# Layer 0 of a two-layer trunk, from mixer to experts: C by SyncE, gate row a tile earlier, table turns behind the router, B tables behind the overflow row

## The reference, cut to what matters

```python
def reference(x, c, positions, ada_w, ada_b, ...):
    cond = jax.nn.silu(c)
    for layer in range(DEPTH):
        mod = cond @ ada_w[layer] + ada_b[layer]
        sh_m, sc_m, g_m, sh_f, sc_f, g_f = jnp.split(mod, 6, axis=-1)
        h = _modulate(_rmsnorm(x, norm_mix_g[layer]), sh_m, sc_m)
        if layer % 2 == 0:
            m = _attn_lru_mixer(h, positions, ...)
        else:
            m = _s5_mixer(h, ...)
        x = x + g_m[:, None, :] * m
        h = _modulate(_rmsnorm(x, norm_ffn_g[layer]), sh_f, sc_f)
        x = x + g_f[:, None, :] * _hier_moe(h, ...)
    return _rmsnorm(x, final_g)
...
    # in _s5_mixer: B is scaled by coefficients of the poles, C is used as it is
    bb_re = coef_re[..., None] * br - coef_im[..., None] * bi
    bu_re = jnp.einsum('bsgc,gpc->bsgp', u, bb_re)
    y = (jnp.einsum('bsgp,gcp->bsgc', h_re, c_re) - jnp.einsum('bsgp,gcp->bsgc', h_im, c_im) + d * u)
```

## Time and profile before

| | |
|---|---|
| median of 3 runs | 955.0 us (953.03 to 955.36) |
| the profiled execution's own time | 954.5 us |
| its span | 952.7 us, 12757 instructions |
| mean granted TensorE clock | 0.956 of full |
| TensorE matmul busy | 848.1 us (89%) |
| VectorE, ScalarE, GpSimd busy | 303.4, 191.3, 150.9 us |
| chain that ended last | TensorE 75%, VectorE 10%, DMA 7% |
| of it the load of C's imaginary part | 3% |
| HBM read | 279.50 MB, 299 GB/s over the span |

### The profile page before, as it was taken

The page is one execution under the profiler, slowest core; times in us unless marked ns, Lnnn a source line. Parts: engine busy times, 40 slices in busy tenths (PEclk is TensorE's granted clock), DMA queues, the critical chain, the costliest instruction groups (busy, mean ns, idle before and its releaser), DMA issues.

```text
span 952.7 us, 12757 instructions
## 1 busy us (share of the span) xinstructions
PE 848.1 (89%) x5229; PEld 463.9 (49%) x5230; DVE 303.4 (32%) x708; ACT 191.3 (20%) x310; POOL 150.9 (16%) x244
## 2 busy tenths in 40 slices
PE   3799998799999998999687999699999899999993
PEld 0367644565465553554544543434444554654641
DVE  1337432541130410311799610620000311301314
ACT  1403330421221311312400100310101212213111
POOL 3201019185443445300000000000000000000000
PEclk9799999789999999999799999789999899999997
DMA  9999999439999999996997682207775299999961
GB/s 306 346 382 276 343 384 360 164 130 400 392 399 402 393 398 400 392 392 245 395 337 263 214 310 87 98 2 259 275 261 186 106 398 392 396 397 391 393 248 68
DMA packets 126288, 285.32 MB, mean 299 GB/s; under 512 B 7092, under 2 KB 8388, under 8 KB 125992
## 3 DMA queue, kind: packets, MB, share of 16 engines
q1 hardware_dynamic: 119392, 276.83, 78.9%
q0 software_dynamic: 1984, 5.21, 1.9%
q10 hardware_dynamic: 4872, 2.72, 1.0%
HBM read 279.50 MB, written 5.24 MB: 299 GB/s over the span
## 4 chain that ended last, share of the span: by engine, by line
PE 75%; DVE 10%; DMA 7%; ACT 2%; issue 2%; SPq 2%; ACTq 1%; DVEq 0%
PE PS L1578 19%; PE PS L1597 13%; PE PS L1605 8%; PE PS L1621 7%; PE PS L1581 6%; PE PS L1866 5%; PE PS L1324 4%; PE PS L1418 3%; DMA yg<-in_s_c_im 3%; DMA ring<-in_moe_w 2%; DMA work<-in_ada_w 2%; PE PS L1349 2%; DVE work L1289 2%; PE PS L1401 2%; SPq L339 1%
## 5 line engine op out<-in xcount | busy, mean ns | idle before, releaser
L1597 PE MATMUL PS<-ring,work 128*64 128x512 f32 (+1 forms) x512 | 130.5, 597 | 6.2 <-ACT work L772 6.2
L1578 PE MATMUL PS<-ring,hT 128*64 128x256 f32 x896 | 108.4, 383 | 2.5 <-DMA ring<-in_moe_w 2.5
L1578 PE MATMUL PS<-ring,yg 128*64 128x256 f32 x896 | 107.4, 381 | 0.0
L1578 PEld LDWEIGHTS PS<-ring,hT 128*64 128x64 f32 x896 | 66.5, 137 | 40.0 <-issue 8.5
L1597 PEld LDWEIGHTS PS<-ring,work 128*64 128x64 f32 (+1 forms) x512 | 43.1, 143 | 85.4 <-issue 85.4
L1211 DVE TENSOR_TENSOR work<-work,PS 128x512 f32<-128x512 f32 x32 | 22.0, 687 | 194.9 <-PE PS L1578 146.9
L1605 PE MATMUL PS<-work,xhat 128*128 128x256 f32 (+1 forms) x256 | 76.9, 453 | 7.0 <-issue 6.9
L1578 PEld LDWEIGHTS PS<-ring,yg 128*64 128x64 f32 x896 | 68.1, 138 | 29.7 <-issue 0.9
L1215 DVE COPY yg<-PS 128x512 f32<-128x512 f32 x32 | 22.1, 692 | 180.5 <-PE PS L1597 180.5
L1621 PE MATMUL PS<-yg,grow 64*128 64x512 f32 (+1 forms) x256 | 70.1, 612 | 7.1 <-DVE yg L1215 7.1
L1605 PEld LDWEIGHTS PS<-work,xhat 128*128 128x128 f32 x256 | 49.2, 207 | 38.8 <-issue 22.1
(11 more groups left out here) (345 smaller groups left out, 978.3 us busy)
## 6 DMA issues: line engine op xcount, KB each, us to landing
ring<-in_moe_w SPq DMA_DIRECT2D x96, 2048.0 KB, 16.7
ring<-in_ada_w SPq DMA_DIRECT2D x20, 2048.0 KB, 15.0
work<-in_ada_w SPq DMA_DIRECT2D x4, 2048.0 KB, 13.8
ring<-in_s_glu_w SPq DMA_DIRECT2D x4, 2048.0 KB, 16.6
ring<-in_ab_w_in SPq DMA_DIRECT2D x3, 2048.0 KB, 21.9
ring<-in_ab_w_out SPq DMA_DIRECT2D x2, 2048.0 KB, 13.6
rot_tables<-work POOLq DMA_DIRECT2D x16, 256.0 KB, 5.7
ring<-rot_tables SPq DMA_DIRECT2D x2, 2048.0 KB, 11.1
```

The costliest lines, as they stand in the source:

```text
L1578: last = mm(dst[64 * u:64 * u + 64, 0:256], hg[k][:, e * P:e * P + 64], w[:, k, 256 * u:256 * u + 256], start=k == 0, stop=k == KD - 1)
L1597: last = mm(dst, heT[:, at:at + (64 if narrow else P)], w[:, c4, h * HALF:(h + 1) * HALF], start=c4 == 0, stop=c4 == KF - 1)
```

## The change

It moves work in layer 0 between the last closing tiles and the first gather, and nothing is added or left out but waits.

- SyncE issues the four loads of C, behind the last adaLN weights of the early part (and behind `pv_done` 6, when the memory is free), ahead of the first expert weights. ScalarE no longer does.
- `ada_cols(1)` and `gate_row(0)` stand one closing tile earlier, behind tile (0, 0) and (0, 1).
- `turn_tables(0, 4)` stands behind the router's columns and the first opening, into banks 0, 5, 2 and 3. Tables 2 and 3 wait for the copy of the second gate row (`grow_ready` 2). Bank 5 is that of accumulator 1, which is opened last, behind the copy of the tables (`tab_evac` 4); the router no longer waits for it.
- On ScalarE the second gate row is copied ahead of both exponentials, and the table copies behind them, in place of ahead of the norm.
- GpSimd makes the B tables behind `over_row(0)`.
- In layer 1 three banks instead of two are opened ahead of the rank matmuls, and the gate row is copied ahead of the exponentials.

```diff
-        TABLES = ((2, 0, 0, 6), (2, 0, 1, 7), (2, 1, 0, 4), (2, 1, 1, 5),
+        TABLES = ((2, 0, 0, 0), (2, 0, 1, 5), (2, 1, 0, 2), (2, 1, 1, 3),
...
@@ SyncE
                 send_ada(u)
+            sp_.wait_ge(S("pv_done"), 6)
+            for v, name in enumerate(("s5_c_re", "s5_c_im")):
+                for u in range(2):
+                    sp_.dma_start(Cn[:, v, :, u * 64:(u + 1) * 64],
+                                  a[name][0].rearrange("(k g) c p -> (g c) k p", k=KD)).then_inc(S("cn_in"), 16)
             for L in range(2):
                 n0 = MOE_BASE[L]
...
@@ GpSimd
+            over_row(0)
             for tab, c0 in ((G1, 3), (G0, 5)):
...
             pool.sem_inc(S("b_tables"), 1)
 
-
-            over_row(0)
             w32 = lambda m: Ew[:, m, :]
...
@@ ScalarE
             s.activation(lr_t[:, :, :], lr_t[:, :, :], ACT.Sqrt).then_inc(S("lru_a"), 1)
-            for v, name in enumerate(("s5_c_re", "s5_c_im")):
-                for u in range(2):
-                    s.dma_start(Cn[:, v, :, u * 64:(u + 1) * 64],
-                                a[name][0].rearrange("(k g) c p -> (g c) k p", k=KD)).then_inc(S("cn_in"), 16)
             rows_out(1)
             gate_row(0)
...
             def ffn(L):
                 n = 2 * L + 1
-                if L == 0:
-                    table_evac(0, 4)
-                else:
+                if L == 1:
                     s.activation(warm, ones[:, 0:1], ACT.Sqrt)
                 norm(n)
                 modulate(n)
+                gate_row(n)
                 act.wait_ge(S("lg_ready"), L + 1)
                 s.activation(exp_g.rearrange("p (b e) -> p b e", b=NB), sets_b(less)[:, :, 0, :], ACT.Exp).then_inc(
                     S("exp_ready"), 1)
-                gate_row(n)
                 act.wait_ge(S("l2_ready"), L + 1)
                 s.activation(exp_2, mx2, ACT.Exp).then_inc(S("exp_ready"), 1)
+                if L == 0:
+                    table_evac(0, 4)
...
@@ TensorE
             for b, h in tiles:
                 mix_out(b, h, LT, KD)
+                if (b, h) == (0, 0):
+                    ada_cols(1)
                 if (b, h) == (0, 1):
-                    ada_cols(1)
-                if (b, h) == (1, 0):
                     gate_row(0)
...
                     if n_ == 2:
-                        pe.wait_ge(S("grow_ready"), 1)
+                        pe.wait_ge(S("grow_ready"), 2)
...
-            turn_tables(0, 4)
             pe.wait_ge(S("x_new"), 1)
...
                 if L == 0:
                     pe.wait_ge(S("small_in"), 16 * 9)
-                    pe.wait_ge(S("tab_evac"), 4)
...
-                open_acc(0)
-                open_acc(1)
+                for m in (0,) if L == 0 else (0, 1, 2):
+                    open_acc(m)
+                if L == 0:
+                    turn_tables(0, 4)
                 pe.wait_ge(S("member_ready"), L + 1)
...
                 last.then_inc(S("rank_ps"), 1)
-                open_acc(2)
-                open_acc(3)
+                for m in (2, 3) if L == 0 else (3,):
+                    open_acc(m)
+                if L == 0:
+                    pe.wait_ge(S("tab_evac"), 4)
+                    open_acc(1)
                 pe.wait_ge(S("narrow_known"), L + 1)
```

## The result

The change takes **949.93 us** (median of 6 runs, 945.86 to 950.24) against 953.83 (6 runs, 952.47 to 955.36) for the kernel before: ratio **0.995**, 95% interval [0.993, 0.997]. A second series on another chip gave 947.89 (6 runs, 947.31 to 951.04), ratio 0.9947 [0.9929, 0.9966]. The profiled execution took 948.89 us with a span of 947.1 (before: 954.5 and 952.7). The forecast was 949.0 in a range of 945.5 to 952.5. The total was right, in part by luck. The kernel before measured 953.83 and not the 955.0 that the forecast set out from, so the gain is 3.9 us by the medians (5.4 in the second series), where 6.0 was forecast. In the profiles two errors work against each other: the first gather began 6.8 us earlier and not 5.2, and 3.2 us of that went again in the experts' stage, where nothing was to be lost.

A forecast was written before the change was run, and what follows sets the result against it. The bound was the chain of waits in layer 0 up to the first gather, including C's load (23.91 us). Gather 5.2 earlier plus 0.6 shorter: 954.5 - 5.8 = 948.7, with 0.5 to the median, rounded 949.0; range 945.5 to 952.5.

The forecast's parts named there:

- Residual, x, norm: Layer 0 behind the closing tiles: residual starts 3.6 us earlier, x ready 3.1 earlier, norm 5.8 earlier.
- C: C's loads on SyncE: landing between 149.8 and 172.5, wanted by TensorE at 176.7, so cost nothing.
- Router to gather: Layer 0, turned x to first gather: rank matmuls at 179.3, gather 5.2 us earlier and 0.6 shorter.
- From there to the end of the router's matmuls 8.2 us stay: From x's turns at 167.55, the router's matmuls take an unchanged 8.2 us, ending at 175.7.
- I expect the fall near 181.5: TensorE's clock falls to 0.50 near 181.5, after dense work ends at 178.7, during the openings.
- I take 185.0 for the gather's start: First gather of layer 0 starts at 185.0, 5.2 us earlier, between picks at 184.2 and openings at about 185.5.
- rival 1: The clock holds through openings and gather: gather at 184.2 in 8.11 us, gain 8.7, time 946.3 or 945.9; chance 0.08.
- Tables beside the first group: GpSimd's B tables beside VectorE's first-group work: cost nothing, at worst 1 us, from 0.36 an operation for three operations.
- GpSimd's end: GpSimd's last work of layer 0 moves to about 403, needed some 459: cover of 56 us, cost nothing.
- The experts' stage: Weights' stream starts when the first slot is freed, so equally earlier: no loss, bounds plus and minus 0.5 us.
- Layer 1: One more opening ahead of rank matmuls, gate row ahead of the exponential: taken 0, bounds 1.9 gained, 0.3 lost.
- The sum: Whole kernel: 954.5 less 5.8 makes 948.7, with 0.5 to the median and rounded 949.0.

The follow-up runs named there:

- experiment 8: Kernel before, with only the four table turns, their copies and the openings moved behind the router (layer 1 as in the change): 949.82 us, ratio 0.9962.
- experiment 7: The change with B tables held until the first group's weights are turned, gate row and its columns back in their old place: 948.87 us, ratio 0.9948.
- Experiment 6: The change, with C's loads issued by ScalarE as before instead of SyncE: 949.91 us, ratio 0.9967.
- Experiment 9: Openings' zero products over 128 rows instead of one: 942.55 us on the change with B tables held (945.90 without), 950.23 on the kernel before.
- experiment 5: The change, with GpSimd's last twelve products (H0 table) held until the fourth group's weights are turned: 947.37 us, ratio 0.9946.
- experiment 1: The change, with GpSimd making the B tables ahead of the overflow row again: 949.36 us, ratio 0.9958.
- experiment 2: The change, with the B tables on GpSimd held until TensorE has turned the first group's weights: 945.90 us, ratio 0.9931.
- experiment 3: The kernel before, with only the B tables moved behind the overflow row: 956.21 us, ratio 1.0039.
- experiment 4: The change, with each of the B tables' sixteen GpSimd operations cut into two of half the columns: 946.14 us, ratio 0.9929.
- tables held: The change, with GpSimd's B tables waiting until TensorE has turned the first group's weights: 945.90 us, ratio 0.9931.

## Why the prediction was right, and where not

**Residual, x, norm: right.** Forecast were a residual 3.6 us earlier, x 3.1 and turns of x 5.8. Net of the 0.59 they are 3.4 (157.02 against 161.05), 3.1 (164.13 against 167.82) and 5.8. The additions took 0.69, as taken. Of the turns of x, experiment 8 gives 2.7 to the table turns, experiment 7 gives 1.7 to the gate row, and the rest of 1.4 is left for the tables.

**C: right.** Its loads landed 14.4 us (the real part, median of two) and 6.0 us (the imaginary part) after their issues from 125 and from 136 on, and nobody waited. Experiment 6 shows that who issues it is of no account.

**Router to gather: undersized.** "From there to the end of the router's matmuls 8.2 us stay" failed: it was 7.0. The turns of x began while the clock was still at the higher level (2.95 us and not 3.65), and it was back during the router (0.72 in 170 to 172). That is partly the luck of the profile: in the second profile of the change the turns took 3.65 and the stretch 7.7, and its gather came at 37.56 and not 36.81. "I expect the fall near 181.5" came true. But by then the openings were all but done, because the rank matmuls had begun at 177.58 and not at 179.3, so "I take 185.0 for the gather's start" came out at 182.81, or 183.4 net. The picks were last, as in rival 1, while the gather itself ran at the lower clock, as forecast (10.42 with 10.1 taken). The forecast took the low clock at the gather as given, once the dense work ends. Experiment 9 shows that it hangs on the one-row openings ahead of the gather: with full rows it ran at 1.00. The clock stayed at 1.00 over the turns of C and for some 4 us behind them. By the Trainium skill ("TensorE: Matmul & The Clock Gate", section PE-mode transpose) transposes don't count for the clock in the same way. The trace disagrees as far as it reaches: sixteen of them ran in 1.97 us at 1.00, and the clock didn't fall behind them. No run has the change without the turns in this place, so that they held the clock up is not shown.

**Tables beside the first group: wrong.** The step was "TensorE wants its results only some 10 us behind the gather. Nothing; at worst 1, by an estimate from those 0.36 for three operations that count". Eight operations count, and each loses 0.88 us and not 0.36: 9.53 against 2.51, of which 3.29 reach TensorE as a wait. At the experts' end that wait is worth 0.8 (experiment 5), so the bound held, but not for the reason given. The addition in the earlier trace rows was a poor measure. It lost 0.14 to 0.53 us for 0.69 of its own, with other work between one and the next; the comparisons follow each other every 0.27 us, and one of them got through for each product. Experiments 1, 2, 3 and 4 show this from four sides. VectorE's copies from PSUM (L1200) take 0.81 us beside the tables and in the kernel before alike. The Trainium skill ("GPSIMD Engine Reference", section Specifications) names the class: GpSimd shares its SBUF interfaces with VectorE, for instructions in a 2-port perf mode or with two SBUF inputs. The trace agrees for the additions (two SBUF inputs, 0.69 to 1.05) and for the sources in PSUM; which mode the comparisons run in, no record here shows.

**GpSimd's end: near in time (399.3, with 403 forecast), wrong as "cost nothing".** I looked at who needs GpSimd's last work, and not at whom it would run beside on its way. The H0 products came to lie on the fourth group's comparisons: 3.05 us of wait, and 2.9 at the experts' end (experiment 5). This is the larger of the two errors.

**The experts' stage: wrong, "no loss, bounds plus and minus 0.5".** It lost 3.2 us. The two waits make 6.3; about half was no loss, since before TensorE stood for the weights' stream instead. That is mostly the first group's wait. The reading that the stream starts with the first freed slot was right, and carries the gain.

**Layer 1: forecast 0, bounds 1.9 gained and 0.3 lost; 0.8 lost in this pair of profiles**, ahead of the gather's end, where TensorE spends 3.80 us in issue and not 2.12. From the S5 states to the first block behind the gather, the three profiles with layer 1 as before take 172.4 to 173.8 us and the eleven with it as changed 173.2 to 174.8. The two overlap, so a loss isn't shown, and no gain either.

**The sum.** Net of the start, 6.8 at the gather less 3.2 in the stage make 3.7 at the experts' end (303.35 to 299.69). The profiled executions differ by 5.6, with 0.6 of start and 2 of clock behind the experts, less 0.8 in layer 1. The medians of the two series differ by 3.9 and 5.4, so 5.8 was forecast, and some 4 to 5 are the change's. That the total of 949.0 lies within 1 us of the 949.93 measured owes 1.2 us to the kernel before, which measured 953.83 and not 955.0.

**What the parts are worth.** Table turns 3.1 us at the experts' end (experiment 8). Gate row 2.5 (experiment 7), where GpSimd is out of the way. With the tables still ahead nothing of it can be measured: the version of experiment 1, which adds the gate row and C on SyncE to the turns alone, ends at 300.75, and the turns alone at 300.27. C nothing. The tables' new place loses 2.8 when put into the kernel before, and 3.65 against tables held; both figures hold the wait in the fourth group, which the longer queue of GpSimd brings with it. The version of **942.55 us** beats both kernels: the change, tables held, openings over full rows.

## What to carry to other kernels

Work moved to an idle engine isn't free because its result is wanted late: ask what the other engine does at that time. Beside GpSimd's long operations, short VectorE comparisons on SBUF got through here only once for each GpSimd operation; move such work, hold it for a few us, or cut it into shorter operations. Look for it also where a queue of later work slides along behind the part that was moved.

A stage whose weights' stream is full is as long as the stream. Bring its first request forward, and don't count stalls inside it at full price: an early one was mostly absorbed (0.8 of 3.3 us), a late one was not (2.9 of 3.05).

Where TensorE opens banks with zero products just ahead of dense work, try them over full rows; here it was worth 3.0 to 3.4 us in two kernels. Take the price of such a product from a measured row (0.94 us here) before you fill a wait with it.

## What the runs showed of the hardware

- A VectorE comparison of 128x128 in SBUF takes 0.27 us alone (2.13 for eight), 1.19 beside GpSimd products of 1.05 to 1.3 us and 0.72 beside products of 0.62 to 0.79: it gets through once per GpSimd operation.
- Three zero products of 512 columns over one row and over 128 rows take the same time at the higher clock (2.84 and 2.82 us). Behind the one-row ones the gather began at a granted clock of 0.50 and took 9.5 to 10.7 us in eleven profiles; behind the others it took 8.07, in all three.
- Sixteen turns of 128x128 take 1.91 to 1.97 us at 1.00 and 3.65 at 0.50.
- A product of 128x128 by 512 columns in float32 takes 0.94 us at 1.00 (three in 2.82).
